# Fill matmuls in the norm waits, sines issued later, wider up-projection groups: a two-layer hybrid decoder on one core

## The chip, the core and the metric

One core of a Trainium2 chip. The metric is the device time of one launch in microseconds (us). The engines are PE (TensorE, matmuls; PEld is its weight loads), DVE (VectorE), ACT (ScalarE), POOL (GpSimd) and SP (SyncE, which only issues DMAs here).

## What is computed

Two post-norm layers over 512 tokens and 1024 features, in float32:

```
h = x @ w_in                                   # one projection, split in column groups
y_a = dsa_attention(...)                       # indexer scores, keep the top 128 keys, 8 heads on one k/v head
qb  = (rms_norm(cq, q_norm_g) @ w_uq)          # 384 -> 8 heads x 96: mixer B's queries
kvb = (rms_norm(ckv, kv_norm_g) @ w_ukv)
y_b = causal_attention(q_full, k_full, v_b)
y_c = conformer_conv(conv_in, ...)             # GLU, causal depthwise conv of width 31, LN, swish
merged = sum of gates[i] * (y_i @ w_branch[i])
x = layer_norm(ALPHA * x + merged @ w_out)     # norm 0
ffn = (silu(f_gate) * f_up) @ w_ffn_out
x = layer_norm(ALPHA * x + ffn + ple)          # norm 1
```

## The kernel before

Activations are kept features by tokens: eight blocks of 128 features by 512 tokens. Every float32 product is made of three matmuls: operand and weight are each split in a high part (`wh`, `xh`) and a rest (`wl`, `xl`), and high x high, high x low and low x high are summed in PSUM. This runs through the whole program.

**Weights** come as numbered tiles of 128 x 1024 (512 KB), in the order in which PE uses them. SP loads tile t into one of two raw buffers once the low part of tile t-2 is made (`lo_ready`, L418); ACT copies it to `wh` (`high`, L524), three tiles ahead of PE (`LEAD = 3`) and never before PE has given back the slot of tile t-4 (`tile_used`); POOL subtracts to get `wl` (`low`, L451). `wh` and `wl` have four slots each. PE waits for `lo_ready` of its tile.

**Start.** ACT converts the first tile and the eight blocks of x; tiles 1 and 2 stand between them in its order. Then it waits for the rotary angles of DVE, takes sine and cosine (L662 to L664), and only then goes on to `high` of tile 3 in the loop over `FRONT`. 14 warm-up matmuls (L1072) run on PE ahead of the first tile.

**Front of a layer** (`FRONT`, an order written out by hand and walked by PE and ACT): token groups `idx`, `cq`, `ckv`, `qa` in tiles 0 to 13, two convolution inputs in tiles 14 to 17, mixed with the indexer's transposes and logits; then mixer B's up-projections: `uq` in four groups of 192 columns (a tile each, three k-blocks) and `ukv` in two groups of 512, then conv inputs 2 and 3 (tiles 24 to 27). In a token group the x block is the stationary operand and the weight columns are streamed, for each k-block over four token blocks and three products. `group_out` counts the four evictions by ACT of each group. DVE turns the logits into scores, then runs 12 of the 16 rounds of top-8 search and replace (`select`, six steps a round) and between them the rotations and `conv_input(2)`, after round 9.

**Attention** (`attention_steps`): 64 units (16 heads by four query blocks), each with a slot in PE's, ACT's and DVE's order. PE fills the slots with the gate projections (`part`). DVE does in a slot the mask and maximum (L1274), a reciprocal, the low parts (L1288), every second slot the sum of a value product (`combine`, L1296, which gives a PSUM bank back), some taps of the depthwise convolution (`TAPS_AT`, L1310), and in slots 0 to 11 the last four select rounds. In slot 12 (`KEEP_SLOT`) it also makes the key mask (L1367).

**Norms** (DVE `norm`, PE `norm`): after the last output block DVE adds it (L1387), sums (L1423), PE makes mean and mean square by token (`by_token`, one column each, L1036) and spreads the mean (L1046), DVE and ACT make 1/sd, PE spreads it (L1050), and DVE scales block after block (L1459), ACT adds the bias and writes `xh` (L643), DVE writes `xl` (L1465). In DVE's order `xl` of block j-1 comes after the scaling and centring that belong to block j. In norm 0 PE has the embedding projection between these steps; in norm 1 it has nothing.

Of the kernel before, what the change touches and what calls it, by code (L numbers as in the profile page):

```python
# [25 lines left out]
P = 128  # L26
# [41 lines left out]
TOKEN_GROUPS += [("uq", 192, 3, 1)] * 4 + [("ukv", 512, 2, 1)] * 2  # L68
# [19 lines left out]
STAT = (0, 6)  # L88
FIRST = 452
# [30 lines left out]
for _slot in range(UNITS):  # L120
    _n = 1 if _slot < KEEP_SLOT else 3 if (_slot - KEEP_SLOT) % 6 == 5 else 2
    TAPS_AT.append(range(_taps, min(_taps + _n, CK * CW)))
    _taps = TAPS_AT[-1].stop
# [110 lines left out]
def build(nc, x_t, ple_t, pos, freq, weights, params, out):  # L234
    with ExitStack() as ctx:
# [273 lines left out]
        def _(act):  # L509
# [152 lines left out]
            act.wait_ge(angles, 2)  # L662
            nc.scalar.activation(sin[:], rope_tmp[:, 1, 0:192], ACT.Sin).then_inc(tables, 1)
            nc.scalar.activation(cos[:], rope_tmp[:, 2, 0:192], ACT.Sin).then_inc(tables, 1)  # L664
            act.wait_ge(consts_ready, 8)
            for layer in range(L):
                first = layer * TILES
                for kind, n in FRONT:
                    if kind == "first half":
                        continue  # L670
                    if kind == "tile":
                        if layer == 0 or n > 0:
                            high(n + LEAD, first)
                        if n == 1:

                            act.wait_ge(x_ready, layer * 16 + DK)
                            act.dma_start(par[:], params[layer]).then_inc(
                                par_loaded, 16)
                            act.dma_start(praw[:], ple_t[layer]).then_inc(
                                ple_loaded, 16)  # L680
# [21 lines left out]
                        if n in (7, 9):  # L702

                            src, c, nn = (h_cq, QL, 0) if n == 7 else (h_ckv, KVL, NT)
                            for b in range(NT):

                                act.wait_ge(group_out, layer * 40 + (8 if n == 7 else 12))
# [117 lines left out]
        def _(pe):  # L825
# [25 lines left out]
            def group(t, layer, first):  # L851
# [3 lines left out]
                if part == 0:  # L855
                    if g >= 2:
                        pe.wait_ge(group_out, layer * 40 + 4 * (g - 1))
# [12 lines left out]
                for kk in range(nk):  # L870
                    k = nk * part + kk
                    if g == 0:
                        pe.wait_ge(x_ready, layer * 16 + (k + 1))
                        if layer == 0 and k == 1:
                            arrived(t, first)
                    for b in range(NT):
                        o = psum[:, 4 * (g % 2) + b, 0:ncol]
                        th_, tl_ = src_h[:, k0 + k, b * P:b * P + P], src_l[:, k0 + k, b * P:b * P + P]
                        nc.tensor.matmul(o, th_, h[:, kk], start=(k == 0), stop=False)  # L879
                        nc.tensor.matmul(o, th_, lw[:, kk], start=False, stop=False)  # L880
                        last = nc.tensor.matmul(o, tl_, h[:, kk], start=False, stop=(k == nk * tiles - 1))  # L881
                last.then_inc(tile_used, 1)

            def scratch(n, layer):
# [5 lines left out]
                if n == 0:  # L890
                    pe.wait_ge(group_out, layer * 40 + 12)
                    pe.wait_ge(roped_idx, layer * 2 + 2)
# [137 lines left out]

            def norm(layer, n, before=None, between=None):
# [8 lines left out]
                if before is not None:  # L1040
                    before()
                pe.wait_ge(sum_ready, layer * 2 + (n + 1))
# [4 lines left out]
                if between is not None:  # L1047
                    between()
                pe.wait_ge(diag_ready, layer * 2 + (n + 1))
                nc.tensor.matmul(scale, ones_1[:], sums[n][:, 1], start=True, stop=True).then_inc(spread, 1)  # L1050

# [22 lines left out]
            for layer in range(L):  # L1074
                first = layer * TILES
                for kind, n in FRONT:
# [4 lines left out]
                    else:  # L1081
                        j, value = CONV_PLACE[n]
                        if n == T_CONV:
                            pe.wait_ge(group_out, layer * 40 + 16)
                        if j >= 1:
                            pe.wait_ge(conv_in if value else conv_th, layer * CK + j)
                        if j == 2:
                            pe.wait_ge(group_out, layer * 40 + 36)
                        half = {"first half": range(DK // 2), "tile": range(DK // 2 if n == T_CONV + 3 else 0, DK)}[kind]
                        project(n, first, xh, xl, DK, [(6 if j < 2 else 0) + value], ks=half)  # L1090
                pe.wait_ge(group_out, layer * 40 + 40)
# [87 lines left out]
        def _(dve):  # L1179
# [196 lines left out]
            def norm(layer, n, start, tile):  # L1376
# [78 lines left out]
                for j in range(DK + 1):  # L1455
# [7 lines left out]
                    if 1 <= j <= DK and not last:  # L1463
                        dve.wait_ge(x_high, x0 + (DK + j))
                        v.scalar_tensor_tensor(xl[:, j - 1], u[:, j - 1], column(b, j - 1), xh[:, j - 1].bitcast(F32),  # L1465
                                               ALU.add, ALU.subtract).then_inc(x_ready, 1)

            dve.sem_inc(passed, 1)
            for layer in range(L):
# [4 lines left out]
                dve.wait_ge(group_out, layer * 40 + 4)  # L1474
# [6 lines left out]
                dve.wait_ge(group_out, layer * 40 + 8)  # L1481
# [14 lines left out]
                dve.wait_ge(group_out, layer * 40 + 16)  # L1496
# [46 lines left out]
                for n, step in enumerate(SELECT[:6 * SELECT_FRONT]):  # L1543
# [3 lines left out]
                    if n == 6 * 7 - 1:  # L1547
                        dve.wait_ge(group_out, layer * 40 + 32)
                        x = uq[:].rearrange("p t (h d) -> p t h d", h=BH)[:, :, :, BN:BQ]
                        rope(x, BH, BR // 2, AD // 2, x, roped_u, layer * 2 + 2)  # L1550
                    if n == 6 * 9 - 1:
# [141 lines left out]
def weight_tiles(w_in, w_uq, w_ukv, w_branch, w_out, w_ffn_in, w_ffn_out, w_ple_gate, w_ple_proj):  # L1693
# [11 lines left out]
    tiles += [token_tiles(w_uq[:, 192 * g:192 * g + 192], 192, 3) for g in range(4)]  # L1705
# [66 lines left out]
```

## Time and profile before

| | us |
|---|---|
| median of 3 runs | 1872.09 (1871.52 to 2578.71) |
| the profiled execution | 1868.89 |
| its span | 1867.1 |
| PE busy in the span | 1821.4 |
| mean granted clock of PE | 0.992 of full speed |

The span is the time from the first to the last instruction; what the execution takes around it is 1.8 us. Of the three runs two lie within 0.6 us; the third is far off. "Busy" adds up instructions, so that a PE that is fed without a pause is busy though it may wait in the array; the granted clock says at which share of its full rate it ran.

### The profile page before, as it was taken

The numbers are of one execution on the slowest core, as the hardware profiler recorded it, in microseconds if no ns is written. First come the engines' busy times: TensorE is split into PE (matmuls) and PEld (weight loads), VectorE is DVE, ScalarE is ACT, GpSimd is POOL, SyncE is SP. The second block draws the span as 40 slices with busy tenths as digits, with TensorE's granted clock in tenths as the row PEclk, the third lists the DMA queues.
The fourth block names the chain that finished last, engine by engine and source line by source line (L and its number), as shares of the span: only waits on it lengthen the run. The fifth ranks groups of instructions, "written<-read, shape, count | busy, mean of one in ns | idle before, by whom it ended". The sixth has DMA issues, their size and how long they took to land.

```text
span 1867.1 us, 25340 instructions
## 1 busy us (share of the span) xinstructions
PE 1821.4 (98%) x8732; PEld 1503.4 (81%) x8732; DVE 1049.0 (56%) x1949; ACT 811.6 (43%) x1447; POOL 770.7 (41%) x338
## 2 busy tenths in 40 slices
PE   8999999999999999999999999999999999999996
PEld 8888788877778888887798887888777888888875
DVE  5289999868973111102253999997889721112023
ACT  4544777743333222222344457777424323222222
POOL 4444223344454444443533432233544544444531
PEclk9999999999999999999999999999999999999998
DMA  5332111223233333332333221112232333333322
GB/s 183 94 99 85 53 57 57 62 75 91 92 111 102 91 100 100 91 103 81 115 99 91 91 87 50 58 57 68 79 102 79 104 103 98 94 97 101 101 81 78
DMA packets 47033, 166.06 MB, mean 89 GB/s; under 512 B 5472, under 2 KB 5728, under 8 KB 46944
## 3 DMA queue, kind: packets, MB, share of 16 engines
q1 hardware_dynamic: 46080, 163.60, 29.1%
q10 hardware_dynamic: 864, 1.28, 0.2%
q8 instruction: 55, 0.90, 0.2%
q14 instruction: 34, 0.28, 0.0%
HBM read 162.76 MB, written 2.10 MB: 88 GB/s over the span
## 4 chain that ended last, share of the span: by engine, by line
PE 35%; issue 35%; POOL 18%; DVE 7%; ACT 4%; DMA 1%; POOLq 0%; DVEq 0%; SPq 0%; ACTq 0%
POOL sb_wl L451 17%; PE banks L828 6%; PE banks L830 6%; PE banks L829 6%; PE banks L879 3%; PE banks L881 3%; PE banks L880 3%; PE banks L935 2%; PE banks L985 2%; DVE banks L1310 1%; ACT sb_pbuf L562 1%; DVE sb_pbuf L1274 1%; DMA sb_wraw<-in_weights 1%; ACT sb_wh L524 1%; ACT sb_pbuf L569 1%
## 5 line engine op out<-in xcount | busy, mean ns | idle before, releaser
L451 POOL TENSOR_TENSOR sb_wl<-sb_wraw,sb_wh 128x1024 fp32r<-128x1024 f32 x303 | 743.1, 2456 | 1057.7 <-ACT sb_wh L524 1057.5
L828 PE MATMUL banks<-sb_xh,sb_wh 128*128 128x512 f32 x1344 | 540.5, 402 | 2.8 <-POOL sb_wl L451 1.8
L830 PE MATMUL banks<-sb_xh,sb_wl 128*128 128x512 f32 x1344 | 525.0, 391 | 0.0
L829 PE MATMUL banks<-sb_xl,sb_wh 128*128 128x512 f32 x1344 | 524.3, 390 | 0.0
L524 ACT ACTIVATE sb_wh<-sb_wraw 128x1024 fp32r<-128x1024 f32 x303 | 319.0, 1055 | 260.6 <-PE banks L830 142.9
L830 PEld LDWEIGHTS banks<-sb_xh,sb_wl 128*128 128x128 f32 x1344 | 252.2, 188 | 54.2
L828 PEld LDWEIGHTS banks<-sb_xh,sb_wh 128*128 128x128 f32 x1344 | 253.1, 188 | 53.0 <-issue 5.1
L829 PEld LDWEIGHTS banks<-sb_xl,sb_wh 128*128 128x128 f32 x1344 | 253.1, 188 | 41.7
L1310 DVE SCALAR_TENSOR_TENSOR banks<-sb_hconv,sb_par,banks 128x512 f32<-128x512 f32 x232 | 172.2, 742 | 1.3
L828 PE MATMUL banks<-sb_hh,sb_wh 128*128 128x512 f32 x352 | 139.3, 396 | 2.1 <-POOL sb_wl L451 2.1
L830 PE MATMUL banks<-sb_hh,sb_wl 128*128 128x512 f32 x352 | 138.1, 392 | 0.0
L829 PE MATMUL banks<-sb_hl,sb_wh 128*128 128x512 f32 x352 | 136.8, 389 | 0.0
L1387 DVE TENSOR_TENSOR sb_u<-sb_u,banks 128x512 f32<-128x512 f32 x32 | 21.9, 685 | 201.5 <-PE banks L830 201.3
L1664 DVE TENSOR_TENSOR sb_th<-sb_th,banks 128x512 f32<-128x512 f32 x44 | 30.2, 688 | 175.6 <-PE banks L830 175.6
L1661 DVE SCALAR_TENSOR_TENSOR sb_th<-sb_th,banks 128x512 f32<-128x512 f32 x44 | 30.3, 688 | 158.2 <-ACT sb_th L528 158.2
L802 ACT ACTIVATE sb_hh<-sb_th 128x512 f32 x44 | 27.8, 632 | 203.7 <-DVE sb_th L1664 203.7
L528 ACT ACTIVATE sb_th<-banks 128x512 f32<-128x512 f32 x60 | 35.8, 597 | 176.3 <-PE banks L830 176.3
L879 PE MATMUL banks<-sb_wh,sb_xh 128*128 128x452 f32 (+3 forms) x256 | 90.4, 353 | 6.6 <-DVE sb_xl L1465 3.5
L880 PE MATMUL banks<-sb_wl,sb_xh 128*128 128x452 f32 (+3 forms) x256 | 90.3, 353 | 0.0
L881 PE MATMUL banks<-sb_wh,sb_xl 128*128 128x452 f32 (+3 forms) x256 | 90.2, 352 | 0.0
L562 ACT ACTIVATE sb_pbuf<-sb_pbuf,sb_small 128x128 f32<-128x128 f32 (+3 forms) x128 | 71.6, 559 | 24.7 <-DVE sb_small L1274 23.8
L828 PEld LDWEIGHTS banks<-sb_hh,sb_wh 128*128 128x128 f32 x352 | 66.2, 188 | 16.7 <-issue 3.4
(290 smaller groups left out, 2970.6 us busy)
## 6 DMA issues: line engine op xcount, KB each, us to landing
sb_wraw<-in_weights SPq DMA_DIRECT2D x304, 512.0 KB, 3.6
sb_u<-in_x SPq DMA_DIRECT2D x8, 256.0 KB, 6.2
out<-sb_u SPq DMA_DIRECT2D x8, 256.0 KB, 2.0
sb_praw<-in_ple ACTq DMA_DIRECT2D x2, 512.0 KB, 3.9
sb_par<-in_params ACTq DMA_DIRECT2D x2, 98.5 KB, 1.9
sb_rope_tmp<-in_freq ACTq DMA_DIRECT2D x1, 24.0 KB, 4.5
sb_small<-in_pos ACTq DMA_DIRECT2D x1, 2.0 KB, 4.2
```

The costliest lines, as they stand in the source:

```text
L451: nc.gpsimd.tensor_tensor(wl[:, t % WS, :], wraw[:, t % 2, :], wh[:, t % WS, :].bitcast(F32), ALU.subtract).then_inc(lo_ready, 1)
L524: nc.scalar.activation(wh[:, t % WS, :], wraw[:, t % 2, :], ACT.Copy).then_inc(hi_ready, 1)
L562: nc.scalar.activation(pbuf[:, n % 3, 0:w], pbuf[:, n % 3, 0:w], ACT.Exp, scale=-1.0, bias=nmax[:, n % 4:n % 4 + 1], accum_out=psums[:, n ...
L828: nc.tensor.matmul(out, wh_, xh_, start=start, stop=False)
L829: nc.tensor.matmul(out, wh_, xl_, start=False, stop=False)
L830: return nc.tensor.matmul(out, wl_, xh_, start=False, stop=stop)
L879: nc.tensor.matmul(o, th_, h[:, kk], start=(k == 0), stop=False)
L880: nc.tensor.matmul(o, th_, lw[:, kk], start=False, stop=False)
L881: last = nc.tensor.matmul(o, tl_, h[:, kk], start=False, stop=(k == nk * tiles - 1))
L935: last = nc.tensor.transpose(psum[0:rows, bank, b * P:b * P + P], src, ident[:])
L985: last = nc.tensor.matmul(psum[:, bank, q0:256], v, pt[half][:, b, q0:256], start=(i == 0), stop=(i == len(passes) - 1))
L1310: steps.done(v.scalar_tensor_tensor(acc, h, w, acc, ALU.mult, ALU.add))
```

## The change

- `fill(n, bank)`: n matmuls of `ones_c` by `ident` (128 x 128 x 128, float32) into a PSUM bank that nobody reads. In norm 0 three stand ahead of the wait for the sum; in norm 1 six stand there, three ahead of the wait for 1/sd, and nine behind its spread (in the last layer the nine are left out).
- The sines of layer 0 move in ACT's order from ahead of `FRONT` to behind `high` of tile 4 (the fifth tile), ahead of the loads of `par` and `praw`, which stood there already.
- `uq` goes in two groups of 384 columns and two tiles each: the first tile of a group holds two k-blocks, the second the third one and zeros, which `GROUP_K` keeps PE from multiplying. The number of tiles stays; `group_out` counts 32 a layer in place of 40.
- `conv_input(2)` moves from behind select round 9 to behind round 8. Slot 12 has one tap in place of two, and of the later slots every fifth (in place of every sixth) has three.
- In norm 1, DVE writes `xl` of block j directly after scaling it, one step earlier than before; in norm 0 the order stays.

```diff
-TOKEN_GROUPS += [("uq", 192, 3, 1)] * 4 + [("ukv", 512, 2, 1)] * 2
+TOKEN_GROUPS += [("uq", 384, 2, 2)] * 2 + [("ukv", 512, 2, 1)] * 2
+GROUP_K = {"idx": DK, "cq": DK, "ckv": DK, "qa": DK, "uq": QL // P, "ukv": KVL // P}
+OUTS = NT * len(TOKEN_GROUPS)
...
+FILL, FILL_BANK = ((3, 0, 0), (6, 3, 9)), (7, 4)
...
-    _n = 1 if _slot < KEEP_SLOT else 3 if (_slot - KEEP_SLOT) % 6 == 5 else 2
+    _n = 1 if _slot <= KEEP_SLOT else 3 if (_slot - KEEP_SLOT) % 5 == 4 else 2
...
-            act.wait_ge(angles, 2)
-            nc.scalar.activation(sin[:], rope_tmp[:, 1, 0:192], ACT.Sin).then_inc(tables, 1)
-            nc.scalar.activation(cos[:], rope_tmp[:, 2, 0:192], ACT.Sin).then_inc(tables, 1)
...
                         if n == 1:
-
+                            if layer == 0:
+                                act.wait_ge(angles, 2)
+                                nc.scalar.activation(sin[:], rope_tmp[:, 1, 0:192], ACT.Sin).then_inc(tables, 1)
+                                nc.scalar.activation(cos[:], rope_tmp[:, 2, 0:192], ACT.Sin).then_inc(tables, 1)
...
-                for kk in range(nk):
+                for kk in range(min(nk, GROUP_K[name] - nk * part)):
...
+            def fill(n, bank):
+
+                for _ in range(n):
+                    nc.tensor.matmul(psum[:, bank, 0:P], ones_c[:], ident[:], start=True, stop=True)
...
                 if before is not None:
                     before()
+                fill(FILL[n][0], FILL_BANK[n])
                 pe.wait_ge(sum_ready, layer * 2 + (n + 1))
...
                 if between is not None:
                     between()
+                fill(FILL[n][1], FILL_BANK[n])
                 pe.wait_ge(diag_ready, layer * 2 + (n + 1))
                 nc.tensor.matmul(scale, ones_1[:], sums[n][:, 1], start=True, stop=True).then_inc(spread, 1)
+                if layer < L - 1 or n == 0:
+                    fill(FILL[n][2], FILL_BANK[n])
...
-                    if 1 <= j <= DK and not last:
-                        dve.wait_ge(x_high, x0 + (DK + j))
-                        v.scalar_tensor_tensor(xl[:, j - 1], u[:, j - 1], column(b, j - 1), xh[:, j - 1].bitcast(F32),
-                                               ALU.add, ALU.subtract).then_inc(x_ready, 1)
+                    i = j - (n == 0)
+                    if 0 <= i < DK and not last:
+                        dve.wait_ge(x_high, x0 + (DK + i + 1))
+                        v.scalar_tensor_tensor(xl[:, i], u[:, i], column(b, i), xh[:, i].bitcast(F32), ALU.add,
+                                               ALU.subtract).then_inc(x_ready, 1)
...
-                    if n == 6 * 9 - 1:
+                    if n == 6 * 8 - 1:
                         conv_input(2)
...
-    tiles += [token_tiles(w_uq[:, 192 * g:192 * g + 192], 192, 3) for g in range(4)]
+    rows = np.concatenate([w_uq, np.zeros((P, w_uq.shape[1]), w_uq.dtype)], axis=0)
+    tiles += [token_tiles(rows[:, 384 * g:384 * g + 384], 384, 2) for g in range(2)]
```

## Rows read from the trace of the kernel before

**Rows 1.** The page, part 1, and of part 5 the costliest line and mean ns.
```profile
PE 1821.4 (98%) x8732; PEld 1503.4 (81%) x8732; DVE 1049.0 (56%) x1949; ACT 811.6 (43%) x1447; POOL 770.7 (41%) x338
...
L451 POOL TENSOR_TENSOR sb_wl<-sb_wraw,sb_wh 128x1024 fp32r<-128x1024 f32 x303 | 743.1, 2456 | 1057.7 <-ACT sb_wh L524 1057.5
```

**Rows 2.** Waits of PE: us in total, times, longest.
```profile
PE banks L1036 <- DVE sb_sums L1423: 4.6, 4, 1.5
```

**Rows 3.** Timeline of the start: start us, us, engine, line, operation [idle before <-releaser].
```profile
21.53 0.36 ACT L663 ACTIVATE sb_sin<-sb_rope_tmp 128x192 f32<-128x192 f32 x1 [4.98 <-DVE sb_rope_tmp L1243]
...
22.05 1.04 ACT L524 ACTIVATE sb_wh<-sb_wraw 128x1024 fp32r<-128x1024 f32 x1
...
25.57 0.48 PE L879 MATMUL banks<-sb_wh,sb_xh 128*128 128x452 f32 x1 [3.05 <-POOL sb_wl L451]
```

**Rows 4.** Windows: us, PE, PEld, DVE, ACT, POOL busy (instructions), granted clock, DMA, GB/s.
```profile
25.00:30.00 5.00, 4.43 (x15) 3.93 (x16) 0.60 (x1) 0.69 (x1) 2.86 (x2) 0.68 0.61 147
924.00:939.00 15.00, 11.41 (x35) 8.13 (x36) 11.30 (x22) 5.77 (x9) 2.35 (x1) 0.66 0.18 64
1424.00:1431.00 7.00, 6.68 (x27) 4.71 (x28) 3.57 (x9) 2.93 (x5) 2.39 (x1) 0.76 0.15 61
```

**Rows 5.** Timeline of PE: first matmuls of the runs of 416, 256, 512, 192, 512 columns.
```profile
32.14 0.35 PE L879 MATMUL banks<-sb_wh,sb_xh 128*128 128x416 f32 x1
...
50.25 0.28 PE L879 MATMUL banks<-sb_wh,sb_xh 128*128 128x256 f32 x1
...
61.77 0.40 PE L879 MATMUL banks<-sb_wh,sb_xh 128*128 128x512 f32 x1
...
115.88 0.25 PE L879 MATMUL banks<-sb_wh,sb_ch 128*128 128x192 f32 x1
...
131.94 0.41 PE L879 MATMUL banks<-sb_wh,sb_ch 128*128 128x512 f32 x1
```

**Rows 6.** Windows of the selects and the first slots, layer 0 (columns as in 4).
```profile
117.00:165.00 48.00, 48.00 (x281) 42.00 (x280) 47.65 (x121) 18.25 (x36) 26.00 (x11) 1.00 0.37 111
167.00:222.00 55.00, 52.37 (x289) 43.48 (x288) 52.75 (x137) 38.57 (x91) 14.34 (x6) 1.00 0.19 58
```

**Rows 7.** Timeline around the first attention slots of layer 0, DVE and PE.
```profile
166.70 1.29 DVE L1319 TENSOR_TENSOR sb_k_l<-banks,sb_k_h 32x512 fp32r<-32x512 f32 x2 [1.51 <-ACT sb_k_h L540]
...
169.23 2.53 DVE L1338 TENSOR_TENSOR sb_ukv_r<-sb_ukv,sb_ukv_r 128x256 fp32r<-128x256 f32 x1
...
213.93 0.75 DVE L1310 SCALAR_TENSOR_TENSOR banks<-sb_hconv,sb_par,banks 128x512 f32<-128x512 f32 x1
...
216.69 0.63 PE L935 MATMUL banks<-sb_ident,sb_pbuf 128*128 128x128 f32 x4 [1.26 <-DVE sb_yb L1296]
...
223.27 0.69 DVE L1274 CUSTOM_DVE_ANT_0 sb_pbuf<-banks,sb_causal 128x512 f32<-128x512 f32 x1 [1.23 <-PE banks L963]
```

**Rows 8.** Line L1338 in the whole run: count, ns min/median/max, first and last start.
```profile
L1338 DVE TENSOR_TENSOR sb_ukv_r<-sb_ukv,sb_ukv_r x16: 404/407/2541, 169.2 to 1181.3; 128x256 fp32r<-128x256 f32 x16
```

**Rows 9.** Timeline of norm 1 of layer 0 and the first tile behind it.
```profile
924.06 3.17 PE L1036 MATMUL banks<-sb_ones_d,sb_sums 128*128 128x1 f32 x16 [1.51 <-DVE sb_sums L1423]
...
931.02 0.75 DVE L1459 SCALAR_TENSOR_TENSOR sb_u<-sb_u,sb_par,banks 128x512 f32<-128x512 f32 x1 [0.55 <-PE banks L1050]
...
931.80 0.72 ACT L643 ACTIVATE sb_xh<-sb_u,sb_par 128x512 fp32r<-128x512 f32 x1 [3.02 <-DVE sb_u L1459]
...
933.54 0.74 DVE L1465 SCALAR_TENSOR_TENSOR sb_xl<-sb_u,sb_par,sb_xh 128x512 fp32r<-128x512 f32 x1
...
934.43 0.44 PE L879 MATMUL banks<-sb_wh,sb_xh 128*128 128x452 f32 x1 [3.53 <-DVE sb_xl L1465]
```

**Rows 10.** Timeline of norm 0 of layer 0, then of the last norm.
```profile
504.84 1.02 PE L1050 MATMUL banks<-sb_sums,sb_ones 128*128 128x512 f32 x2
...
1849.30 1.95 PE L1036 MATMUL banks<-sb_ones_d,sb_sums 128*128 128x1 f32 x16 [1.50 <-DVE sb_sums L1423]
...
1852.84 1.99 PE L1050 MATMUL banks<-sb_sums,sb_ones 128*128 128x512 f32 x2 [0.63 <-DVE sb_sums L1447]
...
1854.94 0.75 DVE L1459 SCALAR_TENSOR_TENSOR sb_u<-sb_u,sb_par,banks 128x512 f32<-128x512 f32 x1 [0.97 <-PE banks L1050]
```

More of the change, by code:

```diff
@@ L705, in _ @@
                             for b in range(NT):
-                                act.wait_ge(group_out, layer * 40 + (8 if n == 7 else 12))
+                                act.wait_ge(group_out, layer * OUTS + (8 if n == 7 else 12))
                                 act.wait_ge(ssq_ready, layer * 8 + (nn + b + START))
@@ L856, in group @@
                     if g >= 2:
-                        pe.wait_ge(group_out, layer * 40 + 4 * (g - 1))
+                        pe.wait_ge(group_out, layer * OUTS + 4 * (g - 1))
                     if g == 4:
@@ L880, in group @@
                         nc.tensor.matmul(o, th_, lw[:, kk], start=False, stop=False)
-                        last = nc.tensor.matmul(o, tl_, h[:, kk], start=False, stop=(k == nk * tiles - 1))
+                        last = nc.tensor.matmul(o, tl_, h[:, kk], start=False, stop=(k == GROUP_K[name] - 1))
                 last.then_inc(tile_used, 1)
@@ L890, in scratch @@
                 if n == 0:
-                    pe.wait_ge(group_out, layer * 40 + 12)
+                    pe.wait_ge(group_out, layer * OUTS + 12)
                     pe.wait_ge(roped_idx, layer * 2 + 2)
@@ L1083, in _ @@
                         if n == T_CONV:
-                            pe.wait_ge(group_out, layer * 40 + 16)
+                            pe.wait_ge(group_out, layer * OUTS + 16)
                         if j >= 1:
@@ L1087, in _ @@
                         if j == 2:
-                            pe.wait_ge(group_out, layer * 40 + 36)
+                            pe.wait_ge(group_out, layer * OUTS + (OUTS - NT))
                         half = {"first half": range(DK // 2), "tile": range(DK // 2 if n == T_CONV + 3 else 0, DK)}[kind]
                         project(n, first, xh, xl, DK, [(6 if j < 2 else 0) + value], ks=half)
-                pe.wait_ge(group_out, layer * 40 + 40)
+                pe.wait_ge(group_out, layer * OUTS + OUTS)
                 pe.sem_inc(passed, 1)
@@ L1473, in _ @@
                 steps.done(v.tensor_scalar(par[:, 0:HALVED], par[:, 0:HALVED], 0.5, None, ALU.mult))
-                dve.wait_ge(group_out, layer * 40 + 4)
+                dve.wait_ge(group_out, layer * OUTS + 4)
                 for k in range(2):
@@ L1480, in _ @@
                 steps.done(v.memset(hconv[:, :, 0:CW - 1], 0.0))
-                dve.wait_ge(group_out, layer * 40 + 8)
+                dve.wait_ge(group_out, layer * OUTS + 8)
                 rope(h_cq[:, :, QL:QL + BR].unsqueeze(2), 1, BR // 2, AD // 2, key_rope.unsqueeze(2), roped_u,
@@ L1495, in _ @@
                                     ALU.mult).then_inc(normed_c, 1)
-                dve.wait_ge(group_out, layer * 40 + 16)
+                dve.wait_ge(group_out, layer * OUTS + 16)
                 def rope_queries(k):
@@ L1547, in _ @@
                     if n == 6 * 7 - 1:
-                        dve.wait_ge(group_out, layer * 40 + 32)
+                        dve.wait_ge(group_out, layer * OUTS + (OUTS - 2 * NT))
                         x = uq[:].rearrange("p t (h d) -> p t h d", h=BH)[:, :, :, BN:BQ]
                         rope(x, BH, BR // 2, AD // 2, x, roped_u, layer * 2 + 2)
-                    if n == 6 * 9 - 1:
+                    if n == 6 * 8 - 1:
                         conv_input(2)
```

## The prediction, made before the changed kernel was run

> **What bounds the kernel now.** I read the page first: PE is busy 1821.4 of 1867.1 us, the other engines 41 to 56% [rows 1]. So time comes back only from PE's own work, from its idle time, and from stretches at half clock. PE's waits and the timeline give the idle time that the change touches: 3.05 us for tile 3's low part at the start [rows 3], 1.26 for a value sum in attention [rows 7], 3.53 for `xl` behind norm 1 [rows 9], and 4.6 us ahead of the norms' sums in four waits [rows 2], of which 1.51 and 1.50 are norm 1's [rows 9, 10], so that the two norms 0 have 0.8 each. The windows show the granted clock: 1.00 (2.4 GHz) nearly everywhere, at the lower level (1.2 GHz) in parts of three stretches behind such gaps: 5 us at the start with a mean of 0.68, 15 us in and behind norm 1 of layer 0 with 0.66, and 7 us in norm 0 of layer 1 with 0.76 [rows 4]. In norm 0 of layer 0, with the same gap, L1050 ran at full speed (1.02 us for its two passes, 1.99 in the last norm [rows 10]). So whether the clock falls hangs on more than the gap, and I can give it only a chance.
>
> **The start (sines).** ACT's copy of tile 3 stood behind the sines, which waited for DVE's angles until 21.53, and began at 22.05; POOL's subtraction followed, and PE idled 3.05 us until 25.57 [rows 3]. With the overlap of a stream (a matmul of 416 columns lasts 0.35 us, the next starts 0.19 after it) that is 3.2. Tile 3's 24 matmuls then took until 32.14, 6.57 us [rows 5]; by the step per matmul below (0.204 for 452 columns) 4.9 at full clock: 1.7 us. ACT was free for 4.98 us ahead of 21.53, so from 16.55 at the latest [rows 3]; copy (1.04) and subtraction (2.46, [rows 1]) end by 20.1, over 2 us ahead of PE's 22.4. What is late next: the sines, about 24 if POOL slows DVE's angles; behind them on ACT stand the loads of `par` and `praw` and the copy of tile 5. PE wants tile 5 at 22.4 + 4.9 + 4.5 = 31.8, it would be there by 29; the first rotation follows the eviction of `idx`, about 29. Gain **4.9**. Bounds: 3.2 (the clock falls all the same) and 4.9.
>
> **The queries' up-projection.** 144 matmuls of 192 columns ran from 115.88 to 131.94: 0.1115 us each. 96 of 416 columns took 50.25 - 32.14, 0.189 each, 96 of 256 took 61.77 - 50.25, 0.120 [rows 5]. So 192 columns cost nearly as much as 256. 384 is not in the trace: the line between 256 and 416 gives 0.175 (and 0.204 for 452); bounds are 0.189, and 0.160 for 384 columns at 2.4 GHz. 72 x 0.175 = 12.6 against 16.06: PE has **3.5** us less a layer (2.5 to 4.5). Tiles are now used in 4.2 and 2.1 us by turns; POOL needs 4 x 2.46 = 9.8 for the four in 12.6 and is three tiles ahead at the start, so I cost the unevenness at nothing. With that stock gone each short tile could cost PE what is missing at POOL, 2.46 - 2.1 = 0.4, and the copy's 1.04.
>
> By the Trainium skill, page TensorE: Matmul & The Clock Gate, section Back-to-back issue gap, a matmul of 384 columns would take 384/2.4 GHz + 2.5 ns = 162 ns; by that estimate the saving would be 4.4 us a layer and the total about 1853. The same formula gives 82 ns for 192 columns, where the trace has 111.5 [rows 5]; the page's section on LDWEIGHTS (128 columns at 1.2 GHz, 107 ns) agrees with that row.
>
> **What attention takes of it.** DVE was busy 47.65 of 48 us ahead of attention and 52.75 of 55 in the first slots [rows 6]; PE waits for it at 216.69, and only at 223.27 does DVE wait for PE (1.23) [rows 7]. So until slot 13 DVE sets the time, and PE's 3.5 us arrive only as far as DVE gains too. It gains the 1.51 us for which it waited for PE's first transposes, and 0.75 by the tap that leaves slot 12, which lies ahead of 216.69 [rows 7]: 2.2, the lower bound. It may gain 2.1 more: L1338 at 169.23 took 2.53 against a median of 0.41 [rows 7, 8], the length of a POOL subtraction; with PE earlier, ACT's copy and the subtraction behind it come 3.5 us earlier and are nearly over when DVE gets there. Upper bound: PE's 3.5 and 0.8 off its 1.26, 4.3. I count half of the 2.1: **3.3** a layer, 6.6 in both. `conv_input(2)` costs nothing: PE wants its bank 3.5 us earlier and it comes one round (48/16, 3 us) earlier, with conv input 3's first half between. The other taps move by at most one, later, where DVE has slack.
>
> **Norm 1 of layer 0.** From L1036 to DVE's first scaling: 931.02 - 924.06 = 6.96 us at half clock [rows 9]. The last norm passed its first part at full clock in 1852.84 - 1849.30 = 3.54; L1050 there took 1.99 and DVE followed 2.10 behind its start; with 1.02 that is 1.13 [rows 10]: 4.7 in all, **2.3** less. The order: `xl` of block 0 can start when `xh` ends, 932.52, and not at 933.54 [rows 9]: **1.0** less. The 15 us with a mean clock of 0.66 hold 10.2 us at the lower level [rows 4], some 7 of them before 931, so 3.3 behind the restart, where PE loses half: **1.7**. Together 5.0. DVE then gives a block every 0.78 + 0.72 + 0.75 + handovers = 2.28 us; PE takes 12 x 0.204 = 2.45: covered by 0.17 a block. The copy of tile 4 stands behind the last `xh` on ACT: ready by 4.7 + 8 x 2.28 + 4 = 27 us after L1036, wanted at 4.7 + 2.4 + 4 x 4.9 = 26.7: no more than 0.3 is lost. Fills: L1050's two passes of 512 columns take 1.02, so a fill of 128 at most 0.26, at half clock 0.51. Six are 1.5 us in a gap of 1.5, three 0.8, nine 2.3 of the some 2.7 left after L1050. The one-column products between stay thin; with the 0.3 I take off 0.7: **4.3**. Bounds: 0 (the clock falls, the nine fills at 4.6 us overrun the restart by more than the order's 1.0) and 5.0.
>
> **The other norms.** Last norm: L1050 1.02 for 1.99, up to 1.0; I take **0.5**. Norm 0 of layer 1: 7 us at 0.76 lose 1.7; three fills of 0.26 in a gap of 0.8 may or may not hold it: **0.8**. Norm 0 of layer 0: nothing.
>
> **Sum.** 4.9 + 6.6 + 4.3 + 0.5 + 0.8 = 17.1 us. From the profiled execution's 1868.9 that is 1851.8; the median of the runs was 3.2 above that execution: **1855.0**.
>
> **Rivals.**
> - *DVE binds in attention.* It gains only 2.2 a layer: 1857.2. For it: DVE's two busy windows [rows 6]. Against: most L1338 do not collide [rows 8].
> - *The fills hold no clock.* Then 2.3 + 1.7 - 0.7 of norm 1 and the 1.3 of the others are lost, and the nine fills overrun by 1: 1855 + 5.6 = 1860.6. For it: the clock fell in norm 0 of layer 1 after 0.8 us of idle time, so the sums themselves do not hold it. Against: norm 0 of layer 0.
> - *`uq` brings nothing*: wider matmuls take in proportion, 0.223: 1861.6. The steps for 256 and 416 speak against it.
> - *Slower than before: DVE behind POOL.* All moments of POOL's subtractions shift against DVE's L1338. One full collision costs DVE 2.1 us, until slot 13 PE too. 16 run, their median is free of it [rows 8]; if 14 more collided, 29 us would be lost, 1884; from 9 on (17.1/2.1) the change is no gain. Only some five a layer lie where DVE sets the time.
>
> The Trainium skill, page SBUF — State Buffer, section Who interferes with whom, says that a DVE instruction with two SBUF inputs and a GpSimd one that reads SBUF exclude each other for the whole instruction. L1338 is such a one; its 2.53 us agree.
>
> **Chances.** Forecast 0.66; DVE binds 0.15; fills hold nothing 0.12; `uq` nothing 0.04; slower 0.03. Range 1848 to 1862: the upper bounds (4.9 + 8.6 + 5.0 + 1.0 + 1.6 = 21.1) from 1868.9 give 1848, the lower ones of start, attention and norms (4.9 + 4.4 + 0.5 = 9.8) from 1872.1 give 1862. A measurement of this kernel tells about 2% (37 us) from no change, and nearly all cases lie inside: same 0.96, faster 0.02, slower 0.02.
>
> **What would show it.** Start: no wait near 22 us, clock 1.00. `uq`: 72 starts in 12.6 us a layer. Attention: the first scores 3.5 us nearer to the scores' end, the first mask 2.2 to 3.5; the wait for L1296 no longer than 1.3. Norm 1: 4.7 us from L1036 to L1459, 2.4 to L879, clock 1.00. I am wrong if PE waits for POOL in `uq`, if its waits for L1296 grow by over 1.3 a layer, or if L879 in layer 1 waits for `xl` block after block.

## The result

| | before | after |
|---|---|---|
| median of the runs of the first comparison, us | 1871.8 (4 runs) | 1855.86 (4 runs) |
| ratio | | 0.9928 [0.9916, 0.9939] |
| median when run again | 1870.16 (9 runs) | 1855.69 (5 runs), ratio 0.9927 [0.9914, 0.9941] |
| the profiled execution | 1868.89 | 1862.37 |
| its span, mean granted clock | 1867.1, 0.992 | 1860.6, 0.995 |
| the second profiled execution: span, clock | | 1853.9, 0.998 |

One of the four runs of the kernel before took 2578.71 us; without it their median is 1871.52. The changed kernel is 14 to 16 us faster, inside the predicted range and 0.7 to 0.9 us from the predicted time. I call its two profiles *first after* and *second after*. The first ran 6.7 us longer than the second; much of what follows comes from comparing the two.

The page of the first after, against [rows 1]:

```profile
PE 1819.3 (98%) x8654; PEld 1502.8 (81%) x8654; DVE 1060.6 (57%) x1949; ACT 813.5 (44%) x1431; POOL 773.0 (42%) x338
L454 POOL TENSOR_TENSOR sb_wl<-sb_wraw,sb_wh 128x1024 fp32r<-128x1024 f32 x303 | 745.3, 2463 | 1048.6 <-ACT sb_wh L527 1048.4
```

**Start.** Timeline of the first after (time, duration, engine, line, what; in brackets the idle time before and its releaser), against [rows 3]:

```profile
15.24 1.04 ACT L527 ACTIVATE sb_wh<-sb_wraw 128x1024 fp32r<-128x1024 f32 x1
...
21.00 1.06 ACT L527 ACTIVATE sb_wh<-sb_wraw 128x1024 fp32r<-128x1024 f32 x1 [4.72 <-DMA sb_wraw<-in_weights]
22.14 2.42 POOL L454 TENSOR_TENSOR sb_wl<-sb_wraw,sb_wh 128x1024 fp32r<-128x1024 f32 x1 [2.58 <-ACT sb_wh L527]
25.87 0.36 ACT L677 ACTIVATE sb_sin<-sb_rope_tmp 128x192 f32<-128x192 f32 x1 [2.50 <-DVE sb_rope_tmp L1255]
26.80 1.06 ACT L527 ACTIVATE sb_wh<-sb_wraw 128x1024 fp32r<-128x1024 f32 x1 [0.31 <-issue]
```

The first line is the copy of tile 3, 6.8 us earlier than the one at 22.05 in [rows 3]; the copies at 21.00 and 26.80 are those of tiles 4 and 5, with the sines between them. PE's wait of 3.05 us is gone and the clock is 1.00 (the row of 25:30 further on).

**Up-projection.** Timeline of the first after, PE, the first matmul of each 36 and the first behind them, against [rows 5]:

```profile
111.53 0.34 PE L882 MATMUL banks<-sb_wh,sb_ch 128*128 128x384 f32 x1
...
117.78 0.34 PE L882 MATMUL banks<-sb_wh,sb_ch 128*128 128x384 f32 x1
...
124.02 0.39 PE L882 MATMUL banks<-sb_wh,sb_ch 128*128 128x512 f32 x1
```

72 matmuls in 12.49 us, 0.1735 each; the estimate was 0.175 and 12.6.

**Attention.** Timeline of the first after, DVE's long instructions ahead of the first score, PE's wait for it and DVE's first mask (L1286), then DVE's key mask (L1379) and PE at the value sum, against [rows 7]:

```profile
126.79 2.78 DVE L1207 TENSOR_TENSOR sb_h_qa<-sb_rope_tmp 128x512 f32<-128x512 f32 x1
129.49 2.88 DVE L1208 TENSOR_TENSOR sb_h_qa<-sb_h_qa,sb_rope_tmp 128x512 f32<-128x512 f32 x1
143.92 2.77 DVE L1207 TENSOR_TENSOR sb_uq<-sb_rope_tmp 128x512 f32<-128x512 f32 x1
165.84 0.30 PE L964 MATMUL banks<-sb_k_h,sb_q_h 96*128 96x128 f32 x1 [1.84 <-DVE sb_k_l L1346]
166.56 0.29 DVE L1286 CUSTOM_DVE_ANT_0 sb_pbuf<-banks,sb_causal 128x128 f32<-128x128 f32 x1
208.10 1.88 DVE L1379 TENSOR_SCALAR sb_work<-sb_work 128x1152 f32<-128x1152 f32 x1
210.86 0.63 PE L938 MATMUL banks<-sb_ident,sb_pbuf 128*128 128x128 f32 x4 [1.26 <-DVE sb_yb L1308]
```

and the same instructions of the kernel before that are not in [rows 7] (two rotations, and the key mask, L1367):

```profile
131.13 2.76 DVE L1195 TENSOR_TENSOR sb_h_qa<-sb_rope_tmp 128x512 f32<-128x512 f32 x1
146.67 2.88 DVE L1196 TENSOR_TENSOR sb_uq<-sb_uq,sb_rope_tmp 128x512 f32<-128x512 f32 x1
214.71 1.09 DVE L1367 TENSOR_SCALAR sb_work<-sb_work 128x1152 f32<-128x1152 f32 x1
```

A rotation's instruction of 128 x 512 takes 0.68 us undisturbed. Before, DVE collided twice in the rotations and once in L1338 (2.53, [rows 7]); after, three times in the rotations and not in L1350 (the old L1338, 0.41). PE waits 1.84 us for DVE, which it did not before.

The key mask met POOL before as well. Timeline of the run "three more steps of the gates" (further on), where POOL is idle at that time:

```profile
208.84 0.75 DVE L1379 TENSOR_SCALAR sb_work<-sb_work 128x1152 f32<-128x1152 f32 x1
```

Undisturbed it takes 0.75 us. In the kernel before POOL's subtraction ran from 212.80 to 215.18 and the mask ended 0.62 behind it; in the first after the subtraction ran from 206.97 to 209.36 and the mask again ended 0.62 behind it. The mask was issued 1.91 us into the subtraction before and 1.13 after; it gained nothing by being earlier.

**Norm 1 of layer 0.** Timeline of the first after, against [rows 9]:

```profile
924.37 1.95 PE L1044 MATMUL banks<-sb_ones_d,sb_sums 128*128 128x1 f32 x16 [0.17 <-DVE sb_sums L1435]
929.14 0.75 DVE L1471 SCALAR_TENSOR_TENSOR sb_u<-sb_u,sb_par,banks 128x512 f32<-128x512 f32 x1
931.59 0.44 PE L882 MATMUL banks<-sb_wh,sb_xh 128*128 128x452 f32 x1 [0.55 <-DVE sb_xl L1478]
```

4.77 us from the sums to the first scaling (predicted 4.7), 2.45 from there to the restart (2.4), and a wait of 0.55 for 3.53.

**The clock.** Windows of the first after: busy time of PE, PEld, DVE, ACT, POOL, then PEclk, DMA share, GB/s, against [rows 4]:

```profile
25.00:30.00 5.00, 5.00 (x27) 4.76 (x26) 1.75 (x5) 3.21 (x6) 2.06 (x1) 1.00 0.71 218
496.00:508.00 12.00, 10.38 (x36) 7.36 (x36) 6.67 (x14) 4.30 (x7) 2.38 (x1) 0.72 0.31 88
918.00:935.00 17.00, 16.28 (x95) 13.68 (x94) 9.95 (x18) 6.53 (x9) 4.77 (x2) 1.00 0.30 92
1089.00:1094.00 5.00, 4.74 (x18) 4.01 (x19) 3.31 (x8) 1.44 (x3) 2.12 (x1) 0.66 0.18 73
1414.00:1424.00 10.00, 9.88 (x53) 7.99 (x52) 8.28 (x14) 4.95 (x7) 2.88 (x2) 1.00 0.36 105
```

and of the second after, the stretches that answer to the second and fourth:

```profile
496.00:503.00 7.00, 7.00 (x36) 5.39 (x37) 4.88 (x11) 3.57 (x6) 2.38 (x1) 1.00 0.15 57
1084.00:1089.00 5.00, 4.84 (x28) 4.31 (x29) 4.56 (x13) 2.62 (x7) 2.27 (x1) 1.00 0.19 72
```

The three stretches of [rows 4] are at full clock. The first after fell to the lower level in two new places, norm 0 of layer 0 and behind the new wait ahead of the first score of layer 1; the second in neither. Behind PE's last matmul both are at the lower level to the end.

**Where the first after lost its 6.7 us.** Timeline of the last output block ahead of norm 0 of layer 0 and of PE's start on its sums, then the same DVE and POOL instructions in the second after:

```profile
471.07 2.39 POOL L454 TENSOR_TENSOR sb_wl<-sb_wraw,sb_wh 128x1024 fp32r<-128x1024 f32 x1 [3.77 <-ACT sb_wh L527]
471.08 2.93 DVE L1646 SCALAR_TENSOR_TENSOR sb_u<-sb_xl,sb_u 128x512 f32<-128x512 f32 x1
...
497.73 2.36 PE L1044 MATMUL banks<-sb_ones_d,sb_sums 128*128 128x1 f32 x16 [1.62 <-DVE sb_sums L1435]
```

```profile
471.48 0.69 DVE L1646 SCALAR_TENSOR_TENSOR sb_u<-sb_xl,sb_u 128x512 f32<-128x512 f32 x1
471.61 2.83 POOL L454 TENSOR_TENSOR sb_wl<-sb_wraw,sb_wh 128x1024 fp32r<-128x1024 f32 x1 [3.44 <-ACT sb_wh L527]
```

In the first DVE issued 0.01 us behind POOL and took 2.93 us for 0.69; in the second it issued 0.13 us ahead, and POOL took 2.83 for 2.39. From there to the norm DVE has no pause that would make it up, so PE waited 1.62 us for its sums, and the clock then fell for 7 us. Going by the same instruction in both profiles, the second after is 0.54 us behind at 464, ahead by 1.84 from 474 on, by 5.12 us behind the norm, and by 6.67 us behind the first scores of layer 1.

**Ledger.** I matched the same instruction in both traces and took the difference of its times (before less second after):

| part | predicted | measured |
|---|---|---|
| start, to 85.91 | 4.9 | 3.8 |
| `uq` and attention, layer 0, to 469 | 3.3 | 1.0 (1.5 at slot 13) |
| norm 0, layer 0 | 0 | 0 |
| norm 1, layer 0, to 1009 | 4.3 | 4.7 |
| `uq` and attention, layer 1, to 1393 | 3.3 | 1.2 (1.5 at slot 13) |
| norm 0, layer 1 | 0.8 | 1.6 |
| last norm | 0.5 | 0.9 |
| sum | 17.1 | 13.2 |

(The start gave 4.3 in the first after; in the second DVE came 0.9 us late with the rotary angles.)

### The profile page after: what moved, and what is told of

Same layout as the page of the kernel before. It is cut to its first block, busy times and chain, and to the rows that moved or that the text cites. A ratio compares the mean times of both kernels' runs of the same rounds, so it can differ in the third digit from the quotient of the medians.

```text
span 1860.6 us, 25164 instructions
## 1 busy us (share of the span) xinstructions
PE 1819.3 (98%) x8654; PEld 1502.8 (81%) x8654; DVE 1060.6 (57%) x1949; ACT 813.5 (44%) x1431; POOL 773.0 (42%) x338
## 4 chain that ended last, share of the span: by engine, by line
issue 38%; PE 30%; POOL 18%; DVE 9%; ACT 4%; DMA 0%; POOLq 0%; DVEq 0%; ACTq 0%; SPq 0%
POOL sb_wl L454 17%; PE banks L831 5%; PE banks L833 5%; PE banks L832 5%; PE banks L882 3%; PE banks L883 3%; PE banks L884 3%; PE banks L938 2%; PE banks L988 2%; DVE sb_work L1270 1%; DVE sb_top L1268 1%; ACT sb_pbuf L565 1%; ACT sb_pbuf L572 1%; DVE banks L1322 1%; DVE sb_pbuf L1286 1%
```

## The experiments

Each was run beside the kernel before, whose medians were 1870.79, 1870.16 and 1869.41 us in the three sessions. For each kernel I give the mean granted clock of its executions. (1 - clock) x span is an estimate of what the lower level cost, an upper one, since a wait loses nothing by it: 17.9 us for before (0.9904), 5.2 for after (0.9972).

**The sines alone.**

```diff
-            act.wait_ge(angles, 2)
-            nc.scalar.activation(sin[:], ...)
...
                         if n == 1:
+                            if layer == 0:
+                                act.wait_ge(angles, 2)
+                                nc.scalar.activation(sin[:], ...)
```

> The kernel before with one edit: ACT's two sines go behind its copy of tile 4. By the prediction's first term 4.9 us less than before (3.2 of idle time and 1.7 at the lower clock); the profile after shows 4.3 at this place. If the sines' new place costs later (ACT's loads of par and praw, the first rotation), less than 4 would arrive.

1869.63 us median of 11, ratio 0.998 [0.9967, 0.9994]. In the profile everything from 62 us on came 4.8 us earlier, nearly the predicted 4.9. Then the last output block lost 2.4 us to a DVE instruction that met POOL (2.90 us at 471.58) and norm 0 of layer 0 fell to the lower clock, as in the first after; behind it the profile was level with before, and 1.2 us later at its end, from the last norm. The term was right at its place and was handed back 400 us later.

**The up-projection alone.**

```diff
-TOKEN_GROUPS += [("uq", 192, 3, 1)] * 4 + [("ukv", 512, 2, 1)] * 2
+TOKEN_GROUPS += [("uq", 384, 2, 2)] * 2 + [("ukv", 512, 2, 1)] * 2
```

> The kernel before with the queries' up-projection in two groups of 384 and nothing else (conv_input(2) and the taps stay where they were). My prediction gave the pair of edits 6.6 us, of which PE's own saving is 7.1. The theory that I now hold (DVE sets the time from the selection to slot 13, so PE's saving turns into PE's wait for DVE): the 1.5 us a layer for which DVE waited for PE's first transposes, less or more 2.1 us for each DVE instruction that meets a subtraction of POOL's, so 0 to 3 us in all, and PE waits 1.5 to 2 us ahead of the first score. The rival (PE's saving arrives and was lost in the profile of after elsewhere): 5.5 to 7 us.

1873.28 us median of 11, ratio 1.0017 [1.0006, 1.0028]: slower than before, outside both expectations. PE did save its 3.5 us a layer. PE's waits in this run (us in total, times, longest):

```profile
PE banks L830 <- DVE sb_hconv L1514: 4.7, 2, 2.4
```

and the windows around them:

```profile
158.00:164.00 6.00, 5.12 (x15) 4.06 (x16) 6.00 (x18) 0.17 (x1) 2.38 (x1) 0.72 0.30 87
1087.00:1093.00 6.00, 4.20 (x12) 3.35 (x13) 6.00 (x18) 1.08 (x2) 2.37 (x1) 0.72 0.29 89
```

PE now waits 2.35 us in each layer for DVE's `conv_input(2)`, still behind round 9, and at that wait the clock fell in both layers; DVE is busy for all of the 6 us. The mean clock of the executions is 0.9879, the lowest of all. DVE met POOL in the rotations three times a layer, as in after, and a fourth time in the instruction that was L1338:

```profile
170.22 2.40 POOL L453 TENSOR_TENSOR sb_wl<-sb_wraw,sb_wh 128x1024 fp32r<-128x1024 f32 x1 [9.60 <-ACT sb_wh L526]
170.39 2.51 DVE L1340 TENSOR_TENSOR sb_ukv_r<-sb_ukv,sb_ukv_r 128x256 fp32r<-128x256 f32 x1
```

The copy ahead of this subtraction stands in ACT's order behind its evictions of PE's first transposes, for which ACT was idle 8.56 us here and 4.28 in the second after. They came late by PE's wait and the half clock behind it, and the subtraction started at 170.22, where it had started at 169.09 before and started at 161.67 in the second after. So DVE gained the 1.5 us of its wait for the transposes and lost 2.2 to the new meeting in the rotations: from the end of the start to slot 13 of layer 0 this profile is 0.7 us slower than before, where the second after is 1.5 faster. The wider groups alone turn PE's saving into waits and lower clock. The move of `conv_input(2)`, which I had costed at nothing, is what I take to make them pay, but no run has the wider groups and this move without the other edits.

**The fills alone.** The functions `fill` and its three calls a norm, on the kernel before.

> The kernel before with the fill matmuls alone. If they hold the clock: norm 1 of layer 0 gives 3.3 (2.3 + 1.7 - 0.7), norm 0 of layer 1 up to 1.6, the last norm up to 0.9: 4 to 5.8 us less in all, and the granted clock is 1.00 in norm 1 of layer 0 and in norm 0 of layer 1. If the hold in after came from other phases of the program and not from the fills, the clock falls there as before and the fills cost up to 1 us.

1865.08 us median of 9, ratio 0.9972 [0.9961, 0.9982]; mean clock 0.9957. In the profile norm 1 of layer 0 gave 3.7 us and norm 0 of layer 1 1.6, with the clock at 1.00 in both; in between a collision of DVE took 2.4 back, and the clock held in norm 0 of layer 1 though PE waited 1.63 us for its sums.

**The order of `xl` alone.**

```diff
-                    if 1 <= j <= DK and not last:
+                    i = j - (n == 0)
+                    if 0 <= i < DK and not last:
```

> The kernel before with the order of xl in norm 1 alone. By the prediction 1.0 us less: xl of block 0 starts when xh ends, one slot earlier, once in layer 0's norm 1. By the rival that xl ahead of the next scaling delays the blocks behind it as much, 0.

1869.16 us median of 11, ratio 1.0003 [0.9994, 1.0012]. Timeline of norm 1 of layer 0 in this run:

```profile
931.61 0.75 DVE L1459 SCALAR_TENSOR_TENSOR sb_u<-sb_u,sb_par,banks 128x512 f32<-128x512 f32 x1 [0.54 <-PE banks L1050]
...
934.04 0.45 PE L879 MATMUL banks<-sb_wh,sb_xh 128*128 128x452 f32 x1 [2.55 <-DVE sb_xl L1466]
```

2.43 us from the scaling to the restart for 3.41 in [rows 9]: the 1.0 is there. In this profile the lower level did not come back behind the restart, so the norm gave 2.6 in all, and norm 0 of layer 1, at the lower level for 6.8 us in place of 3.4, took 1.6 back. In the total none of it shows.

**After without the wider groups.** The kernel that ran is not quite the one that the expectation names: it has the four groups of 192, but `conv_input(2)` stays behind round 8 and the taps stay as in after. So it takes out the wider groups alone.

```diff
-TOKEN_GROUPS += [("uq", 384, 2, 2)] * 2 + [("ukv", 512, 2, 1)] * 2
+TOKEN_GROUPS += [("uq", 192, 3, 1)] * 4 + [("ukv", 512, 2, 1)] * 2
...
```

> The changed kernel with the up-projection in four groups of 192 again and the taps and conv_input(2) in their old places. By my prediction 6.6 us slower than after. By the theory that DVE sets the time up to slot 13: PE does 2 x 3.5 us more work but waits that much less for DVE, and has no wait of 1.8 us ahead of the first score behind which the clock can fall: within 2 us of after, on either side.

1861.23 us median of 5, ratio to before 0.9949 [0.9936, 0.9963]; after in the same session 0.9927 and 1855.69. So in company the wider groups are worth 5.5 us by the medians and 4.1 by the ratios, not within the 2 I expected. This profile is later than the second after by 1.5 us at slot 13 of layer 0, by 1.6 more behind norm 0 of layer 0 (lower clock at 499.9 to 503.3), by 1.5 more in the attention of layer 1 and by 1.0 more in the last norm. The attention itself gives 3.0; the rest is clock. I cannot show that the groups cause that part: the mean clock of the executions is 0.9960 for 0.9972, 2.2 us, but it falls in norm 0 in kernels with the wide groups too (below).

Against the kernel before, this run shows what the other two edits do in attention with groups of 192. DVE, timeline:

```profile
150.44 0.69 DVE L1523 SCALAR_TENSOR_TENSOR sb_hconv<-sb_th_conv,banks 128x512 f32<-128x512 f32 x1 [1.61 <-PE banks L831]
```

That is `conv_input(2)`, a round earlier, waiting for PE: the 1.51 us of [rows 7] have only moved. Up to slot 13 the two edits gave nothing (0.0 us in both layers), and in the later slots 0.4 us a layer were lost.

**A selection round less ahead of attention.**

```diff
-                    select(step, back=2)
+                    if n // 6 != 10:
+                        select(step, back=2)
```

> The changed kernel with the eleventh of the twelve selection rounds ahead of attention left out (six DVE instructions a layer, 2.9 us; so 8 keys fewer are taken for each query of mixer A). If DVE sets the time from the selection to slot 13: PE's wait of 1.8 us ahead of the first score goes, the first score comes 2.9 us earlier, and 2 to 3 us a layer arrive, 4 to 6 in all, and up to 1.7 more from the clock in layer 1. If PE sets it and the 1.8 us are an odd event: the score comes 1.8 earlier at most and PE's later waits take it back, 0 to 2 us in all.

1853.47 us median of 4 (ratio 0.9906 [0.9891, 0.9921]), for a kernel that does less work. The first mask came 2.7 us earlier (164.32 for 167.05 in the second after; 0.7 of it is from the start), PE's wait of 1.8 us was gone, and the two attentions gave 2.1 and 1.7 us in the profile: DVE sets the time there. Both norms 0 then fell to the lower clock and took 1.6 each back.

**Three more steps of the gates ahead of the first score.**

```diff
-    steps += [("part", p) for p in parts[:DK]]
+    steps += [("part", p) for p in parts[:DK + 3]]
```

> The changed kernel with 11 instead of 8 steps of the gates' projections ahead of the first score (so 3 fewer spread over the slots). They are 9 matmuls, 1.8 us, in the place of PE's wait of 1.8 us for DVE. If DVE sets the time up to slot 13, PE has done 1.8 us more by then (less the share of the slots up to 13, a fifth): 1.4 us a layer, 2.9 in all, and up to 1.7 more if the clock no longer falls there in layer 1. If PE sets the time in the slots, nothing changes.

1854.01 us median of 4, ratio 0.9913 [0.9898, 0.9928]. The wait ahead of the first score is gone in both layers, and each attention gave 1.2 us where 1.4 were expected; again both norms 0 fell to the lower clock (1.6 each). By the executions 1.7 us faster than after, but the intervals overlap.

**The rotation after the sixth round.**

```diff
-                    if n == 6 * 4 - 1:
+                    if n == 6 * 6 - 1:
                         rope_queries(1)
```

> The changed kernel with DVE's rotation of mixer A's second four query heads after the sixth selection round instead of the fourth. In every profile with the groups of 384 two of its six instructions met subtractions of POOL's in each layer (2.78 and 2.88 us for 0.68); after the sixth round POOL is idle for most of its 3.6 us (134.56 is its next start). If these meetings are what took the 2.1 us by which DVE no longer collides behind the first transposes: DVE's way to the first score is 2.5 to 4 us shorter a layer, PE's wait of 1.8 us is gone and 3 to 5.5 us arrive in all. If the time of DVE's front does not set the time of the kernel, or the rotation meets POOL as often there: within 1 us of after.

1854.04 us median of 5, ratio 0.9918 [0.9905, 0.9932]. Timeline, DVE, layer 0, and PE's wait ahead of the first score:

```profile
134.07 2.90 DVE L1208 TENSOR_TENSOR sb_h_qa<-sb_h_qa,sb_rope_tmp 128x512 f32<-128x512 f32 x1
142.59 2.90 DVE L1205 TENSOR_TENSOR sb_uq<-sb_uq,sb_cos 128x512 f32<-128x512 f32 x1
165.36 0.30 PE L964 MATMUL banks<-sb_k_h,sb_q_h 96*128 96x128 f32 x1 [1.42 <-DVE sb_k_l L1346]
```

Two meetings with POOL instead of three in layer 0; in layer 1 still three, one of them (L1202, 1.91 us) short of a whole subtraction. I had expected the moved rotation to meet none: DVE reached its last instruction 0.1 us too late, POOL's subtraction had started at 133.95. The attentions gave 0.5 and 0.6 us in the profile (against the second after, the start set aside), less than what I expected and in the right direction.

**No fills.** `FILL = ((0, 0, 0), (0, 0, 0))`.

> The changed kernel without fills. By my prediction 5.6 us slower than after (4.6 in the norms' clock and the others 1.3, less 0.3). If the granted clock of the other parts of the change (start, attention) is what gained, it is within 2 us of after. From the run with the fills alone (5.2 less than before) and the mean granted clocks of its executions (0.9957 for 0.9904): 5 to 10 us slower.

1861.53 us median of 5, ratio 0.9955 [0.9942, 0.9968], mean clock 0.9924: 5.8 us slower than after by the medians, 5.2 by the ratios. The 5.6 of the prediction's rival has 1 us in it for fills that overrun, which a kernel without fills does not have; the same terms without it give 4.6. Windows of norm 1 of layer 0 and of norm 0 of layer 1:

```profile
917.00:934.00 17.00, 12.32 (x44) 8.94 (x43) 13.32 (x24) 6.24 (x9) 2.35 (x1) 0.70 0.20 62
1415.00:1425.00 10.00, 9.16 (x39) 6.50 (x37) 6.75 (x11) 3.36 (x5) 3.99 (x2) 0.83 0.19 57
```

In the profiles norm 1 of layer 0 lost 3.5 us against the second after, norm 0 of layer 1 1.7 and the last norm 0.9. Another 1.9 went in layer 1 from the start to slot 13, with the clock at the lower level behind the wait ahead of the first score, as in the first after; that part need not be the fills'.

**More fills in the norms 0.** `FILL = ((6, 3, 6), (6, 3, 9))`.

> The changed kernel with more fills in the two norms 0: 6 ahead of the sums and 6 behind the spread, 3 between (3, 0, 0 in the change). In norm 0 of layer 0 the clock was at 0.50 for 3.4 to 7 us in four of five profiles of kernels with fills. If fills hold the clock wherever they stand: clock 1.00 in both norms 0, and 0 to 2 us less than after. If they only lengthen the chain there: 1 to 3 us more, as a fill takes 0.28 us and norm 0 has other work of PE's between its steps.

1859.09 us median of 5, ratio 0.9944 [0.9931, 0.9957]: 3.4 us slower than after. The norms 0 held their clock in the profile and lost 0.9 us each, 1.8 of the 3.4: there the fills stand in PE's way. Besides, the clock fell in norm 1 of layer 0 (922 to 926) and behind the first score's wait in layer 1, 1.4 and 1.6 us, and the last norm lost 1.4. Why more fills in norm 0 would bring that is open. I can't tell it from chance with one profile; the executions' mean clock (0.9960) says that it is common in this kernel.

**Three edits together.** The rotation after round 6, 11 steps ahead, and the fills of the run before.

> The changed kernel with three edits together: the rotation after the sixth round, 11 instead of 8 steps of the gates ahead of the first score, and the fills of fill_norm0. If DVE's front sets the time, the rotation alone fills PE's wait and the three steps find no gap left: the gains do not add, 3 to 6 us less than after. If they add: 5 to 8 less.

1854.07 us median of 6, ratio 0.9922 [0.9909, 0.9935]: no better than the rotation alone. But not because the two edits ahead of attention don't add. In the profile the attentions gave 1.5 and 1.3 us against the second after, nearly the sum of the rotation's 0.5 and 0.6 and the gates' 1.2 each; the fills then took 0.9 us in each norm 0. The two edits without the fills were not run. By the medians, nothing I ran that does the whole work beats after by more than 1.7 us.

**The clock over all profiles.** Whether it fell to the lower level:

| stretch | without fills, before among them (5 profiles) | with fills (9 profiles) |
|---|---|---|
| norm 1, layer 0 | 5 of 5 | 1 of 9 |
| norm 0, layer 1 | 5 of 5 | 2 of 9 |
| norm 0, layer 0 | 2 of 5 | 4 of 9 |
| start | 4 of 4 with the sines in front | 0 of 10 with the sines moved |

(The last row goes by the sines, not by the fills.) The kernels of the two columns differ in more than the fills; two pairs differ in the fills alone, after and the run without fills, and the kernel before and the run with the fills alone. The first after fell in norm 0 of layer 0 and the run without fills did not, so for that norm the table shows no use of the fills.

## Why the prediction was right, and where it was not

The time and the range held, the sum did not: 17.1 us forecast, 13.2 found between the two profiles that can be compared. That the median came out within 1 us is in part luck, as the last point but one says: two errors of 3 to 4 us cancelled. And the slow end of the range took 4.9 us for the start, though the start's own lower bound was 3.2.

- **Start: mechanism and place right.** 4.9 forecast; 4.8, 4.3 and 3.8 in three profiles. The sines came at 25.87 and not at 24, which cost PE nothing. What I left out: an earlier start can be lost again at a place that I had costed at nothing.
- **The up-projection on PE: right**, 12.49 us for 12.6. The lower figures in the prediction for 384 columns (0.160 and 162 ns) were not reached, it is 0.1735.
- **What attention takes of it: the term that failed**, 6.6 forecast, 2.2 found. The step was "the lower bound 2.2 a layer, plus half of L1338's 2.1". All of the 2.1 was gained: L1350 takes 0.41. But the same shift of POOL against DVE put two instructions of the first rotation (L1207 and L1208, once L1205 and L1208) in POOL's way instead of one, another 2.1 us, in both layers of each of the seven profiles with the wide groups and the rotation in its old place. So 1.5 a layer were left, the wait for PE's first transposes. The 0.75 of the tap taken from slot 12 went to the key mask (1.88 us for 1.09), which ends with POOL's subtraction whether it starts early or late: PE's wait at the value sum stayed 1.26. And the term that I had at nothing, the other taps and `conv_input(2)`, lost 0.5 and 0.4 us a layer behind slot 13; the run without the wider groups loses as much, so it is not theirs. Which of the two edits does it was not tried. I had priced one instruction's collision and not asked which others the shift would bring about. The rival "DVE binds" was the right picture, and even its 2.2 a layer was too much. The upper bound needed PE's saving to arrive, and PE waited 1.84 us for DVE instead.
- **Norm 1 of layer 0: right**, 4.7 for 4.3, by its steps too; behind the nine fills PE still waited 0.55 us, so they did not overrun.
- **Norm 0 of layer 1: 1.6 for 0.8.** The clock held, and the bound of 1.7 was the value. **Last norm:** 0.9 for 0.5.
- **Norm 0 of layer 0: I said nothing would happen.** It is the least certain place of the program: in the same kernel it cost nothing in one profile and 5.7 us in the other (2.4 by the collision, 3.3 behind it).
- **The 3.2 us between the profiled execution and the median.** I carried them over. Before's executions had a mean clock of 0.9904, its profiled one 0.992: by 1867 us that is 3 us of lower clock that this execution happened to miss. The second after's execution lies at the median of its runs. The change removed the places at which before lost them, so the gain of the medians is larger than that of the profiles, 14.5 to 16 for 13.2. That, and the 1.6 that I had too little in the norms, covered the 4.4 too much in attention and the 1.1 too much in the start.

By the estimate from the mean clocks, up to 12.7 of the 14.5 us are clock (17.9 less 5.2). But 2.5 of that lie in the last norm and behind it, where PE has next to nothing left to do: there the lower level lasts to the end, for 14.1 us before and 9.0 in the second after, and that norm gave only 0.9. So by this estimate some 11 us at most are clock and the rest is work; my sum had 7.0 and 10.1. Taken out of after one at a time, the fills are worth 5.8 us (5.2 by the ratios) and the wider groups 5.5 (4.1). The sines were not taken out of after; at their place they gave 3.8 to 4.8 us, and alone 3.7 in all by the ratio.

Of my slower rival (DVE behind POOL) the mechanism is real, though not where I had put it: one meeting more than before took 2.4 us in the output blocks ahead of norm 0 of layer 0 in three profiles (sines alone, up-projection alone, first after), and each was followed by the lower clock. With the fills alone the same happened in layer 1, and the clock held.

The Trainium skill, page SBUF — State Buffer, section Who interferes with whom, also says that the order of issue decides which of the two blocks, and that a `tensor_scalar` can be caught as well, in its two-port modes, though it has one SBUF input. The traces agree: 0.14 us of issue time, from 0.01 behind POOL to 0.13 ahead, decide between 2.93 and 0.69 us at L1646, and L1379, a TENSOR_SCALAR, took 1.88 us beside POOL and 0.75 without it.

## What to carry to other kernels

Work saved on one engine is worth what the engine that sets the time gains; sum that one's waits and collisions after the shift, not only those that the shift removes. Where the clock falls behind waits, a delay of 2 us on the engine that PE waits for can be paid twice, as a wait and as half speed behind it, so compare the mean clock of all executions and not of one profile. Single edits then don't add up: by their ratios the fills, the sines, the order and the wider groups alone gave 5.2, 3.7, -0.6 and -3.2 us, 5.1 in sum, and the whole change gives 13.7. The wider groups are worth -3.2 us alone and 4.1 in company. So take each edit out of the whole as well as trying it alone.

## What the runs showed of the hardware

- Waits of PE of 0.8 to 3.5 us were often followed by 3.4 to 13.7 us at 0.50 of the clock, but not always. Behind the same wait ahead of the first score (1.81 to 2.13 us, in four profiles) the clock fell in layer 1 in three of them and not in the second after, and in layer 0 (1.83 to 1.87 us) in none. In the norms with fills it fell six times without any wait of 0.2 us or more in the 6 us before (norm 0 of layer 0 at 495.1, 496.6 and 499.9, norm 0 of layer 1 at 1413.3 and 1414.8, norm 1 of layer 0 at 922.3). What tells these apart stayed open.
- Three fills took 0.83 us at full clock (0.28 each). The 33 of the program, some 9 us of PE's time, brought 5.8 us, and the chain beside them became shorter: 4.77 us from the sums to the first scaling in norm 1 of layer 0, 5.73 without fills. The 24 more in the norms 0 cost 0.9 us a norm there, where PE has other work.
- Issue times of DVE and POOL 0.01 to 0.13 us apart decide over 2 us. Those of the rotations were the same in all profiles with the wide groups; the one at 471 us was there in one profile of the changed kernel and not in the other. Why that one varies was not tried.
